# Reordering the first two pairs of a Strassen-like up-projection and the end of a recurrent branch

## The reference, cut to what matters

```python
def conv_ffn(h, w_up, conv_w, conv_b, w_down):       # both layers; h is 1024 x 1024, D_FF = 2816
    z = h @ w_up                                     # 1024 -> 2 * 2816
    zp = jnp.pad(z, ((0, 0), (CONV_W - 1, 0), (0, 0)))
    z = sum(zp[:, j:j + S] * conv_w[j] for j in range(CONV_W)) + conv_b   # 3 taps along the sequence
    gate, up = jnp.split(z, 2, axis=-1)
    return (jax.nn.silu(gate) * up) @ w_down

# partial rotary of branch A: needs cos and sin of position * frequency
rot = jnp.concatenate([x1 * cos - x2 * sin, x2 * cos + x1 * sin], axis=-1)

# branch B: a state per head is carried over 16 chunks
state_next = state * decay[..., None] + chunk_kv
```

## Time and profile before

| | us |
|---|---|
| median of 3 runs | 2197.65 |
| lowest and highest | 2195.17, 2197.65 |
| the profiled execution | 2193.04 |
| its span (first to last instruction) | 2191.2 |

### The profile page before, as it was taken

How to read it: one execution, slowest core, us unless ns; L and a number is a source line. 1 busy time by engine, 2 the same in 40 slices (tenths; PEclk the granted TensorE clock), 3 DMA queues, 4 the chain that set the end, 5 groups by cost and what they waited for, 6 DMA issues and landing times.

```text
span 2191.2 us, 26108 instructions
## 1 busy us (share of the span) xinstructions
PE 2128.9 (97%) x10128; PEld 1738.1 (79%) x10128; DVE 1484.0 (68%) x1679; ACT 887.5 (41%) x1127; POOL 880.4 (40%) x458
## 2 busy tenths in 40 slices
PE   8998999989989999999999999999899999999996
PEld 5886788778868888888888888888688888888885
DVE  6669755463686676777698912436877766686987
ACT  4221233343454444444443532025544444444445
POOL 4323211122267777674000333333777777730000
PEclk9999999999999999999999999999999999999998
DMA  4101000003222222222988211113221222239872
GB/s 164 39 29 39 27 14 29 20 21 115 87 77 87 87 87 87 81 83 90 368 319 288 77 39 39 39 48 119 82 80 67 86 87 87 87 111 381 303 261 77
DMA packets 93916, 236.09 MB, mean 108 GB/s; under 512 B 9937, under 2 KB 10210, under 8 KB 93794
## 3 DMA queue, kind: packets, MB, share of 16 engines
q1 hardware_dynamic: 92642, 230.23, 29.4%
q10 hardware_dynamic: 1152, 4.19, 0.5%
HBM read 198.73 MB, written 35.65 MB: 107 GB/s over the span
## 4 chain that ended last, share of the span: by engine, by line
PE 69%; DVE 4%; ACT 2%; issue 1%; POOL 1%; DVEq 0%; ACTq 0%; POOLq 0%
PE ps L1164 12%; PE ps L1165 11%; PE ps L1166 11%; PE ps L1200 6%; PE ps L1201 6%; PE ps L1198 6%; PE ps L772 3%; PE ps L778 3%; PE ps L775 3%; PE ps L1261 1%; PE ps L1262 1%; PE ps L1263 1%; DVE act_lo L1350 1%; PE ps L1310 1%; DVE t_lo L1705 1%
## 5 line engine op out<-in xcount | busy, mean ns | idle before, releaser
L581 POOL TENSOR_TENSOR w_hi<-w_raw,ones 128x1024 fp32r<-128x1024 f32 x56 | 111.8, 1997 | 799.8 <-PE ps L778 242.3
L1164 PE MATMUL ps<-t_hi,w_hi 128*128 128x512 f32 x672 | 265.4, 395 | 8.0 <-ACT snap L2212 4.8
L1165 PE MATMUL ps<-t_lo,w_hi 128*128 128x512 f32 x672 | 263.0, 391 | 0.0
L1166 PE MATMUL ps<-t_hi,w_lo 128*128 128x512 f32 x672 | 262.6, 391 | 0.0
L627 POOL TENSOR_TENSOR w_lo<-w_sum,w_hi 128x1024 fp32r<-128x1024 f32 x84 | 232.8, 2782 | 23.1 <-ACT w_hi L2215 23.1
L1198 PE MATMUL ps<-d_hi 128*128 128x512 f32 x616 | 240.2, 390 | 0.0
L1201 PE MATMUL ps<-d_hi,d_lo 128*128 128x512 f32 x616 | 239.7, 389 | 0.0
L1200 PE MATMUL ps<-d_lo,d_hi 128*128 128x512 f32 x616 | 239.7, 389 | 0.0
L627 POOL TENSOR_TENSOR w_lo<-w_raw,w_hi 128x1024 fp32r<-128x1024 f32 x84 | 158.3, 1885 | 199.3 <-ACT w_hi L2215 181.5
L1164 PE MATMUL ps<-act_hi,w_hi 128*128 128x512 f32 x504 | 196.8, 390 | 4.6 <-ACT snap L2212 4.6
L1166 PE MATMUL ps<-act_hi,w_lo 128*128 128x512 f32 x504 | 196.6, 390 | 0.0
(11 more groups left out here) (290 smaller groups left out, 4599.9 us busy)
## 6 DMA issues: line engine op xcount, KB each, us to landing
w_raw<-w_up SPq DMA_DIRECT2D x44, 1024.0 KB, 4.9
d_ring<-w_dn SPq DMA_DIRECT2D x146, 256.0 KB, 7.8
d_ring<-g_kept SPq DMA_DIRECT2D x124, 256.0 KB, 9.2
g_kept<-gst SPq DMA_DIRECT2D x44, 512.0 KB, 2.6
w_raw<-w_in SPq DMA_DIRECT2D x24, 512.0 KB, 3.6
chain_a<-g_kept SPq DMA_DIRECT2D x44, 256.0 KB, 8.9
x_kept<-x SPq DMA_DIRECT2D x16, 512.0 KB, 8.7
x<-x_kept SPq DMA_DIRECT2D x16, 512.0 KB, 10.1
```

Of the source, the lines that this page charges most:

```text
L581: pool.tensor_tensor(w_hi[:, slot, :], w_raw[:, parity, :], ones[:, 0:1].to_broadcast([P, 1024]), ALU.mult).then_inc(s_whi, 1)
L1164: pe.matmul(out, wh, bh, start=(fresh and j == 0), stop=False, skip_group_check=True)
L1165: pe.matmul(out, wh, bl, start=False, stop=False, skip_group_check=True)
L1166: ins = pe.matmul(out, wl, bh, start=False, stop=(j == 3), skip_group_check=True)
```

## The change

In the up phases: DVE folds P7's bank and the third snapshot into the snapshot's own buffer as its first step of pair 1 and does the multiplication later, from there, so `taken(1, ...)` swaps C11 and C22. The taps of pair 0 come behind that fold. ACT takes the third snapshot of pair 1 ahead of the starts of pair 0, moves `high_b(2)`, `snap_of(2, 0)`, `start(1, 0)` and `high_c(2)` around the silu of pair 0, and POOL makes the first two sums of pair 2 ahead of `low_a(2)` and `low(1)` ahead of the other two sums. In branch B: `take_gate(1, 1)`, `scan(1, 0)` and `scan(1, 1)` come ahead of `rope_tables`, and the cosines' first DVE instruction is replaced by two activations on ACT.

```diff
         def taken(p, i):
+            if p == 1 and i in (C11, C22):
+                i = C11 + C22 - i
             return 2 + 6 * (p - 1) + i if p else 2
...
                     elif p == 2:
-                        low_a()
                         pool.wait_ge(*past(F.prod, 2))
+                        pool.wait_ge(*past(F.wlo, lows(p - 1, GC)))
...
                     pool.tensor_tensor(sums[:, 0], sums[:, 1], a11, ALU.subtract).then_inc(F.sum.sem, 1)
+                    if p == 2:
+                        low_a()
+                        low(1, sums[:, 0:2], GB)
                     pool.tensor_tensor(sums[:, 2], a11, a21, ALU.subtract).then_inc(F.sum.sem, 1)
...
-                    low(1, sums[:, 0:2], GB)
+                    if p != 2:
+                        low(1, sums[:, 0:2], GB)
...
-                dve.wait_ge(s_rope_a, 2)
-                step(dve.scalar_tensor_tensor(ropeC[:], r_r[:], -2.0, r_r[:], ALU.mult, ALU.mult))
-                step(dve.scalar_tensor_tensor(ropeC[:], ropeC[:], 1.0, rstd[:], ALU.add, ALU.mult))
+                dve.wait_ge(s_rope_a, 4)
+                step(dve.tensor_tensor(ropeC[:], ropeC[:], rstd[:], ALU.mult))
...
             take_by_position(1)
+            take_gate(1, 1)
+            scan(1, 0)
+            scan(1, 1)
             rope_tables()
-            take_gate(1, 1)
...
-            for g in range(3):
-                scan(1, g)
+            scan(1, 2)
...
+                def first_pair():
+                    taps(0, 0)
+                    dve.wait_ge(*past(F.prod, products(1, P2)))
+                    dve.wait_ge(*past(F.snap, 1))
+                    dve.wait_ge(*past(F.tap, 2))
+                    dve.tensor_tensor(fz[:, 0, 0:HALF], ps[:, 3, :], snap[:, 0, :], ALU.add).then_inc(F.ev.sem, 1)
+                    taps(0, 1)
+                    dve.wait_ge(*past(F.tap, 4))
+                    dve.wait_ge(*past(F.ev, taken(1, C22)))
+                    dve.tensor_tensor(fz[:, 1, HALF:S], snap[:, 2, :], rstd[:, HALF:S], ALU.mult).then_inc(F.ev.sem, 1)
+                    dve.wait_ge(*past(F.prod, products(1, P3)))
+                    dve.tensor_tensor(fz[:, 0, HALF:S], ps[:, 2, :], snap[:, 1, :], ALU.add).then_inc(F.ev.sem, 1)
+                    dve.wait_ge(*past(F.ev, taken(1, C12)))
+                    dve.tensor_tensor(fz[:, 0, :], fz[:, 0, :], rstd[:], ALU.mult).then_inc(F.ev.sem, 1)
+                    gate(0)
...
                 first(0)
                 first(1)
-                finish(0)
-                for p in range(1, FT):
+                dve.wait_ge(*past(F.prod, products(1, P7)))
+                dve.wait_ge(*past(F.snap, 3))
+                dve.tensor_tensor(snap[:, 2, :], ps[:, 1, :], snap[:, 2, :], ALU.add).then_inc(F.ev.sem, 1)
+                first_pair()
+                finish(1)
+                for p in range(2, FT):
...
             act.activation(r_r[:], r_a[:], ACT.Sin, scale=0.5).then_inc(s_rope_a, 1)
+            act.wait_ge(s_rope_a, 2)
+            act.activation(ropeC[:], r_r[:], ACT.Square).then_inc(s_rope_a, 1)
+            act.wait_ge(s_rope_a, 3)
+            act.activation(ropeC[:], ropeC[:], ACT.Identity, scale=-2.0, bias=1.0).then_inc(s_rope_a, 1)
...
                 snap_of(1, 1, 1, P6)
+                snap_of(1, 2, 2, P5)
                 start(0, 0)
                 start(0, 1)
-                snap_of(1, 2, 2, P5)
+                high_a(2)
+                high_b(2)
                 silu(0)
-                high_a(2)
-                for p in range(1, FT):
-                    if p > 1:
-                        high_d(p)
-                        start(p - 1, 1)
+                snap_of(2, 0, 0, P1)
+                act.wait_ge(*past(F.silu, 1))
+                start(1, 0)
+                high_c(2)
+                for p in range(2, FT):
+                    high_d(p)
+                    start(p - 1, 1)
+                    if p > 2:
                         snap_of(p, 0, p % 2, P1)
```

More of the change, by code:

```diff
@@ L1759, in finish @@
                 def finish(p):
-                    if p:
-                        dve.wait_ge(*past(F.prod, products(p, P4)))
-                        dve.tensor_tensor(fz[:, 1, 0:HALF], ps[:, p % 2, :], rstd[:, 0:HALF], ALU.mult).then_inc(F.ev.sem, 1)
+                    dve.wait_ge(*past(F.prod, products(p, P4)))
+                    dve.tensor_tensor(fz[:, 1, 0:HALF], ps[:, p % 2, :], rstd[:, 0:HALF], ALU.mult).then_inc(F.ev.sem, 1)
                     taps(p, 0)
@@ L1766, in finish @@
                         d_low(3)
-                    if p:
-                        taps(p, 1)
+                    taps(p, 1)
+                def first_pair():
[13 more added lines that the diff above has]
+                    gate(0)
                 def pair(p):
@@ L1772, in pair @@
                     dve.wait_ge(*past(F.snap, 3 * p - 2))
-                    if p == 1:
-                        dve.wait_ge(*past(F.tap, 2))
                     dve.tensor_tensor(fz[:, 0, 0:HALF], ps[:, 3, :], snap[:, 0, :], ALU.add).then_inc(F.ev.sem, 1)
-                    if p > 1:
[L1777 to L1780, removed]
+                    gate(p - 1)
                     if p == FT - 1:
@@ L1793, in pair @@
                     dve.tensor_tensor(fz[:, 0, :], fz[:, 0, :], rstd[:], ALU.mult).then_inc(F.ev.sem, 1)
-                    if p == 1:
-                        gate(0)
                     if p == FT - 1:
@@ L2210, in snap_of @@
                     if p > 1:
-                        act.wait_ge(*past(F.ev, taken(p - 1, (C11, C12, C22)[i])))
+                        act.wait_ge(*past(F.ev, taken(p - 1, (C11, C12, N22 if p == 2 else C22)[i])))
                     act.activation(snap[:, i, :], ps[:, bank, :], ACT.Copy).then_inc(F.snap.sem, 1)
@@ L2272, in ffn @@
                 snap_of(1, 1, 1, P6)
+                snap_of(1, 2, 2, P5)
                 start(0, 0)
                 start(0, 1)
-                snap_of(1, 2, 2, P5)
+                high_a(2)
+                high_b(2)
                 silu(0)
-                high_a(2)
-                for p in range(1, FT):
-                    if p > 1:
-                        high_d(p)
-                        start(p - 1, 1)
-                        snap_of(p, 0, p % 2, P1)
[L2283 to L2287, removed]
+                snap_of(2, 0, 0, P1)
[6 more added lines that the diff above has]
+                    if p > 2:
+                        snap_of(p, 0, p % 2, P1)
+                    silu(p - 1)
+                    if p < FT - 1:
+                        high_a(p + 1)
+                    snap_of(p, 1, p % 2, P6)
+                    snap_of(p, 2, 2, P5)
                     if p + 1 < FT:
```

## The result

| | before | after |
|---|---|---|
| median of 5 runs, us | 2197.65 | 2183.1 |
| lowest and highest | 2193.89, 2199.55 | 2174.64, 2185.14 |
| the profiled execution | 2193.04 | 2175.4 |
| its span | 2191.2 | 2173.6 |

The ratio is 0.9925, 95% interval 0.9911 to 0.9939: 16.5 us faster by the ratio, 14.6 by the medians, 17.6 between the two profiled executions. The forecast was 18.1 us and 2174.9 for the profiled execution; by the medians it was 2179.5 against 2183.1, inside the range. The profiled execution belongs to the lower heap.

The account below looks back on a forecast made before the run. TensorE, busy 97% of the span, was taken as the bound, so only its waits and half clock could be won. 8.9 + 6.9 + 2.3 = 18.1 us off 2193.04 gave 2174.9, by the median 2179.5; range 2173.5 to 2190.

Parts of the forecast that it names:

- What bounds: Whole kernel: TensorE is busy 97% of the span, so only its waits and half-clock work can be won.
- Up phases: First two pairs of each up phase: 39.45 us, gaining 8.9 us in the first layer and 6.9 in the second.
- The step to P7 of pair 2: Up phases: P7's snapshot on ACT, behind silu(1) and high_a(3), comes late; TensorE waits 1.05 us.
- the rival with both at their slowest: Up phases: both DVE multiplications as slow as the slowest rows; P7 waits 4.5 us, total 2190; chance 0.12.
- Branch B: End of branch B: DVE gains 4.0 us, half clock takes back 1.7, leaving 2.3.
- The term for the clock: End of branch B: half clock behind TensorE's 3.3 us idle piece takes 1.7 us off the gain.
- ScalarE's two activations: Branch B's angles: two activations of some 1.1 us each fit ACT's 4.26 us idle, 2.1 to spare; cost 0.
- an offset of 4.6 us: Whole kernel: median stands 4.6 us above the profiled execution; the same offset turns 2174.9 into 2179.5.
- The queue of ACT: Up phases: ACT's queue makes P7 of pair 2 late, wait 4.5 us plus 1.7 of clock; 2190; chance 0.12.
- the worse rhythm of the later pairs: Up phases, pairs 3 to 21: snapshots 0.55 us later per pair cost 21 us, total 2200.5; chance 0.03.
- replaced one for one: TensorE's waits replaced by waits for the same slow chain; all 18.1 us come back, 2197.6; chance 0.04.
- the rival on branch B: Only branch B's size is off: tables slowed and clock falls, 2183, or clock stays up, 2178; chance 0.15.

Follow-up runs that it names:

- e9: The changed kernel run again, unaltered; ratio 0.9916 to the kernel before, profiled execution 2184.83 us.
- e6: The changed kernel with the snapshot of P6 of pair 2 ahead of silu(1) and high_a(3) on ScalarE; ratio 0.9932 to the kernel before.
- e4: The changed kernel with GpSimd's old order in pair 2 put back; first two pairs 43.54 and 43.37 us in the two layers.
- e1: The kernel before with only the branch B edits (VectorE order, cosines on ScalarE); ratio 0.9997, median 2195.28 against 2195.9 us.
- e5: The changed kernel with the fold of P7 behind the two taps of tile 0 instead of ahead; first two pairs 39.59 and 39.54 us.
- e3: The changed kernel with the first cosine step back on VectorE, ahead of take_gate(1, 1); transposes at 210.84 instead of 210.38 us.

## Why the prediction was right

**What bounds.** It was read from the waits, and the gain came from there: 9.09 us in the first layer's two pairs and 7.14 in the second's (forecast 8.9 and 6.9), 2.16 ahead of the first up phase (forecast 2.3). Between the up phases 0.68 were lost and 0.11 behind them, which the sum had at nothing; 9.09 + 7.14 + 2.16 - 0.68 - 0.11 = 17.6, the difference of the two spans. That the profiled execution came within 0.5 us of the forecast 2174.9 is luck in one respect: before and after both had the short stretch at the end of the attention (370.15 and 370.37 us), and the same kernel in e9 took 2184.83.

**Up phases.** Load, sums, low parts, snapshots and P1 of pair 2 fell within about 0.4 us of where the steps put them, seen from the start of the phase. The step to P7 of pair 2 was right in what is late next (snapshot in ScalarE's queue behind silu and high_a, which hang on VectorE), and e6 showed it by removing it. Its size was 0.77 instead of 1.05. The multiplication that GpSimd holds up took 1.12 where I had put 0.9, and ended 0.55 us behind GpSimd's low part, as in the row that it was taken from; the wide one took 1.60 as put; the rival with both at their slowest did not come about. A wait of 0.77 was not followed by half clock.

**GpSimd.** I gave its reordering no price of its own. e4 shows that without it 4.2 us of the 9.1 of a layer are lost while the rest of the new order stands, more than I saw even when I wrote its expectation: the sums put behind low(1) count as well.

**Branch B.** VectorE reached `take_v` 3.76 us earlier (forecast 4.0), the table instructions took 1.23 and 1.28 (put at 1.2), the idle was 0.79 (put at 0.9). The term for the clock, 1.7 us, was 1.4 in this execution. Over executions it is no constant: 0, 1.4 and 2.6 to 2.8 us by the table. Where it is 2.7, the branch's part is worth 1.1 us, too little for the runs of e1 to tell from nothing. The sum of this part, 2.3 against 2.16, is right for this execution, and partly by luck, as the clock could as well have taken 0 or 2.7: I took one row at 654.85 for what follows a wait of that length.

**ScalarE's two activations** cost nothing, as said: 2.08 us of idle were left where 2.1 were expected, and no table load stood ahead of Square. The Trainium skill, ScalarE: Activation LUTs, What ACT_TABLE_LOAD costs, gives 2.66 us for a switch, with a drain of 1.38 beside the load. The trace doesn't show that drain: the exponential's load starts at 145.71, 1.08 us behind the start of an activation of 1.06, and takes 1.28; the load of silu(0) takes 1.28 from 637.34, and silu starts at 638.63.

**The medians.** 2179.5 was the profiled execution plus an offset of 4.6 us. That offset is not a constant, it was 7.7 after: the profiles of one kernel differ by half clock in several places, 9.4 us in all between the changed kernel's two, and in five runs such draws move the median by several us.

**The rivals.** The queue of ACT was the right suspect with a small size; the worse rhythm of the later pairs did not come: P6 of pairs 4 and 6 of the changed kernel start at 683.62 and 722.06, 38.44 us apart, where it was 38.40. The tables of branch B were not slowed (1.23 and 1.28), and the waits that went were not replaced one for one: TensorE's waits for the snapshots fell from 9.4 to 1.5 us. The 2178 that stands in the rival on branch B holds with unslowed tables and no half clock; slowed tables without half clock would have been 15.8 + 0.35 = 16.15 us of gain, 2181.5.

## What to carry to other kernels

Where one engine is full in steady state, look at the first rounds of each phase: here its waits there were waits for a place in another engine's queue, and an order written out for those rounds alone removed them without a faster instruction. Cost such a change by writing the start of every instruction of the stretch behind its releaser with durations from the trace; here that gave the change's own new waits within 0.3 us, and those of the two variants e4 and e5, costed more briefly, only within 1.2 and 0.8. And judge a change by its own stretch of the profile as well as by the total, when other stretches of the kernel vary by 6 us and more from one execution to the next.

## What the hardware showed that was not expected

The same wait of 3.17 to 3.18 us of TensorE at the same place was followed by no half clock (e6), by a clock of 0.83 over the window of 209 to 219 us (the changed kernel) and of 0.66 (e1, e4, e5, e9). The Trainium skill, TensorE: Matmul & The Clock Gate, section HAM oscillation, ties the fall to idle stretches. These runs agree where it follows waits of TensorE, and add that whether one wait of this length is followed at all differs between executions, worth 0 to 2.8 us here. Near 1265 us (at 1257 to 1275, as the phase comes earlier or later) it followed sixteen matmuls of one column in five profiles of eleven, without any wait in the timeline. Half clock ahead of a wait for another engine costs nothing (e3, and pair 1 of the second layer in e1), so its price depends on where it falls. At the end of the attention, where TensorE has half a dozen waits of 0.4 to 2.5 us, the mean clock of 470 to 515 us was 0.92 or 0.85 (0.89 in e4), and the stretches differ by 6 us, of which 3.2 are the clock itself.
